# The first microseconds of a transformer kernel: a new order for its first loads

## The reference

```python
for i in range(DEPTH):                      # DEPTH = 4, D_MODEL = 1024, SEQ = 256
    h = rmsnorm(x, norm_mix[i])
    if kind == 0: m = mla_mixer(h, positions, w_in[j], q_norm[j], w_uq[j], kv_norm[j], w_ukv[j], w_o[j])
    ...
    x = x + m
    x = x + sq_relu_mlp(rmsnorm(x, norm_mlp[i]), mlp_w1[i], mlp_w2[i])
return rmsnorm(x, norm_final)

def mla_mixer(h, ...):
    proj = h @ w_in                         # 1024 x (256 + 256 + 64)
    c_q, c_kv, k_pe = jnp.split(proj, [256, 512], axis=-1)
    q = rmsnorm(c_q, q_norm) @ w_uq
    kv = rmsnorm(c_kv, kv_norm) @ w_ukv
    # rotary embedding of q_pe and k_pe, causal softmax attention, then @ w_o
```

## Time and profile before

| | us |
|---|---|
| median of 3 runs | 1314.98 |
| the three runs | 1311.99, 1314.98, 1315.52 |
| span of the profiled execution | 1312.0 |
| TensorE busy | 1286.5 |
| VectorE busy | 891.4 |
| ScalarE busy | 671.6 |
| GpSimd busy | 43.5 |

### The profile page before, as it was taken

How to read it: one execution, slowest core, us unless ns; L and a number is a source line. 1 busy time by engine, 2 the same in 40 slices (tenths; PEclk the granted TensorE clock), 3 DMA queues, 4 the chain that set the end, 5 groups by cost and what they waited for, 6 DMA issues and landing times.

```text
span 1312.0 us, 18369 instructions
## 1 busy us (share of the span) xinstructions
PE 1286.5 (98%) x7578; PEld 1126.3 (86%) x7578; DVE 891.4 (68%) x1180; ACT 671.6 (51%) x861; POOL 43.5 (3%) x58
## 2 busy tenths in 40 slices
PE   6999999999999999999999999999999999999998
PEld 5888888888999888887999888888887888888886
DVE  5877666665666666666899886766667876666664
ACT  5555554444555454444776644544445645454442
POOL 3000000000000000000101110000000000000000
PEclk9999999999999999999999999999999999999999
DMA  9744465555845475545574643755554334565540
GB/s 289 143 168 148 141 232 201 193 192 161 233 149 180 132 254 192 192 165 160 181 222 141 203 149 119 249 191 192 191 180 140 117 130 130 168 231 193 192 161 32
DMA packets 146067, 230.93 MB, mean 176 GB/s; under 512 B 7683, under 2 KB 112429, under 8 KB 145984
## 3 DMA queue, kind: packets, MB, share of 16 engines
q1 hardware_dynamic: 143136, 221.66, 50.8%
q0 software_dynamic: 2848, 8.10, 2.9%
HBM read 227.08 MB, written 2.65 MB: 175 GB/s over the span
## 4 chain that ended last, share of the span: by engine, by line
PE 88%; DVE 7%; DMA 1%; issue 1%; ACT 1%; POOL 1%; SPq 0%; POOLq 0%; DVEq 0%; ACTq 0%
PE bank L982 15%; PE acc L902 12%; PE acc L903 12%; PE acc L906 12%; PE bank L987 8%; PE bank L590 7%; PE bank L591 7%; PE bank L592 7%; DVE wlo L573 2%; PE bank L1402 1%; PE bank L1105 1%; PE bank L795 1%; PE bank L1408 1%; PE bank L1090 1%; DMA raw<-in_mla_w_in 1%
## 5 line engine op out<-in xcount | busy, mean ns | idle before, releaser
L573 DVE TENSOR_TENSOR wlo<-raw,whi 128x2048 fp32r<-128x2048 f32 (+2 forms) x207 | 464.7, 2255 | 139.6 <-ACT whi L557 139.5
L557 ACT ACTIVATE whi<-raw 128x2048 fp32r<-128x2048 f32 (+2 forms) x207 | 386.8, 1879 | 45.8 <-PE acc L906 44.2
L982 PE MATMUL bank<-hsplit,whi 128*128 128x512 f32 x896 | 212.2, 389 | 0.0
L903 PE MATMUL acc<-wlo,uhi 128*128 128x512 f32 x512 | 200.1, 391 | 0.0
L902 PE MATMUL acc<-whi,uhi 128*128 128x512 f32 x512 | 199.6, 390 | 0.0
L982 PEld LDWEIGHTS bank<-hsplit,whi 128*128 128x128 f32 x896 | 168.2, 188 | 34.9
L906 PE MATMUL acc<-whi,ulo 128*128 128x512 f32 x512 | 159.2, 390 | 0.0
L590 PE MATMUL bank<-hsplit,whi 128*128 128x256 f32 (+2 forms) x540 | 154.5, 286 | 0.3 <-DVE xn L1980 0.3
L592 PE MATMUL bank<-hsplit,wlo 128*128 128x256 f32 (+2 forms) x540 | 151.4, 280 | 0.0
L591 PE MATMUL bank<-hsplit,whi 128*128 128x256 f32 (+2 forms) x540 | 151.4, 280 | 0.0
L1027 ACT ACTIVATE relu<-bank 128x512 f32<-128x512 f32 x56 | 33.5, 598 | 188.9 <-PE bank L987 188.9
(11 more groups left out here) (252 smaller groups left out, 1813.4 us busy)
## 6 DMA issues: line engine op xcount, KB each, us to landing
raw<-in_mlp_w SPq DMA_DIRECT2D x128, 1024.0 KB, 5.5
raw<-in_ssd_w_in SPq DMA_DIRECT2D x18, 1024.0 KB, 5.4
raw<-in_mla_w_o SPq DMA_DIRECT2D x16, 1024.0 KB, 4.9
raw<-in_mla_w_ukv SPq DMA_DIRECT2D x8, 1024.0 KB, 5.8
raw<-in_moba_w_qkv SPq DMA_DIRECT2D x16, 512.0 KB, 5.3
raw<-in_ssd_w_out SPq DMA_DIRECT2D x8, 1024.0 KB, 4.9
raw<-in_mla_w_uq SPq DMA_DIRECT2D x8, 768.0 KB, 6.0
raw<-in_mla_w_in SPq DMA_DIRECT2D x4, 1024.0 KB, 7.5
```

The lines of the kernel that those rows point to most:

```text
L557: nc.scalar.activation(whi[:, s, lo:e], raw[:, s, lo:e], ACT.Copy).then_inc(w_hi_done[s], 1)
L573: nc.vector.tensor_tensor(wlo[:, s, lo:e], raw[:, s, lo:e], whi[:, s, lo:e].bitcast(F32), ALU.subtract).then_inc(w_split[s], 1)
L903: nc.tensor.matmul(acc[t][half][:], lh, wl[:, k, n], start=False, stop=False)
L982: nc.tensor.matmul(ps, w[0][:, k, m * P:(m + 1) * P], hflat[:, k].rearrange("p a n -> p (a n)"), start=k == 0, stop=False)
```

## The change

SP sends `ident` ahead of the gain. Unit 0 is loaded by two transfers, rows 0 and 1 of its four row groups with a semaphore of their own (`first_half_loaded`), then rows 2 and 3. Before unit 1 SP waits until the second half of unit 0 has landed, and before unit 2 until unit 1 has landed. ScalarE copies the lower half of unit 0 as soon as that half is there, and this copy stands ahead of the copies of tile 0's transposes. POOL computes the power of tile 1 before it issues `relx`, `onehot` and the first latent gains. TensorE's matmuls of `ident` are five and stand ahead of the first transposes.

```diff
--- before.py
+++ after.py
@@ -145,6 +145,7 @@
         ident_loaded = sem("ident_loaded")
         mask_loaded = sem("mask_loaded")
         x_loaded = [sem(f"x_loaded{t}") for t in range(T)]
+        first_half_loaded = sem("first_half_loaded")
         x_ready = sem("x_ready")
         gain_loaded = sem("gain_loaded")
         ssq_done = sem("ssq_done")
@@ -541,6 +542,12 @@
 
         in_halves = (0, 1) if kinds[0] == "mla" else ()
 
+        def act_first_half(act):
+
+            e = units[0][0] * units[0][1]
+            act.wait_ge(first_half_loaded, 16)
+            nc.scalar.activation(whi[:, 0, :e // 2], raw[:, 0, :e // 2], ACT.Copy).then_inc(half_hi_done, 1)
+
         def act_splits(act, key, ahead=AHEAD):
 
             while split_to["act"] < min(first.get(key, key) + ahead + 1, len(units)):
@@ -553,7 +560,8 @@
                 lo = 0
                 if n in in_halves:
                     lo = e // 2
-                    nc.scalar.activation(whi[:, s, :lo], raw[:, s, :lo], ACT.Copy).then_inc(half_hi_done, 1)
+                    if n:
+                        nc.scalar.activation(whi[:, s, :lo], raw[:, s, :lo], ACT.Copy).then_inc(half_hi_done, 1)
                 nc.scalar.activation(whi[:, s, lo:e], raw[:, s, lo:e], ACT.Copy).then_inc(w_hi_done[s], 1)
                 split_to["act"] += 1
 
@@ -664,6 +672,8 @@
             for t in range(T):
                 if not deferred(j):
                     act_sumsq(act, j, t)
+                if j == t == 0 and in_halves:
+                    act_first_half(act)
                 if j < len(stages):
                     act_tr(act, j, t)
                 if j == 0:
@@ -2181,8 +2191,8 @@
                 sp.dma_start(gbc[:], src.to_broadcast([P, DM])).then_inc(gain_loaded, 16)
 
             sp.dma_start(x[:, 0, :], A["x"][0, tok(0), :]).then_inc(x_loaded[0], 16)
+            sp.dma_start(ident[:], A["c_ident"]).then_inc(ident_loaded, 16)
             gains(0)
-            sp.dma_start(ident[:], A["c_ident"]).then_inc(ident_loaded, 16)
             for n, (a, b, srcs) in enumerate(units):
                 s, k = n % SLOTS, n // SLOTS
                 if n == 1:
@@ -2191,9 +2201,17 @@
                     sp.dma_start(mask[:], A["c_mask"]).then_inc(mask_loaded, 16)
                 if n in stage_unit:
                     gains(stage_unit[n] + 1)
+                if n in (1, 2) and in_halves:
+                    sp.wait_ge(raw_loaded[n - 1], raw_count[n - 1])
                 if k:
                     sp.wait_ge(w_split[s], k)
                 w = b // len(srcs)
+                if n == 0 and in_halves:
+                    for half, landed in enumerate((first_half_loaded, raw_loaded[0])):
+                        rows_of = slice(a // 2 * half, a // 2 * (half + 1))
+                        sp.dma_start(raw[:, 0, :a * b].rearrange("p (a b) -> p a b", a=a)[:, rows_of, :],
+                                     srcs[0][:, rows_of, :]).then_inc(landed, 16)
+                    continue
                 for i, src in enumerate(srcs):
                     if isinstance(src, tuple):
                         off, k_rows, width, src = src
@@ -2230,11 +2248,11 @@
                 pool.dma_start(qkvg[:, i, QR:QR + KVR],
                                A["mla_kv_norm"][i:i + 1, :].to_broadcast([P, KVR])).then_inc(qkvg_loaded[i], 16)
 
+            if 0 in norm_index:
+                pool_norm(pool, 0, [1])
             pool.dma_start(relx[0:BUCKETS, :], A["rel_bias"]).then_inc(rel_loaded, 16)
             pool.dma_start(onehot[:], A["c_onehot"]).then_inc(rel_loaded, 16)
             latent_gains(0)
-            if 0 in norm_index:
-                pool_norm(pool, 0, [1])
             pool.wait_ge(raw_loaded[1], raw_count[1])
             latent_gains(1)
             if "ssd" in kinds:
@@ -2298,9 +2316,9 @@
             te.wait_ge(ident_loaded, 16)
             if "moba" in kinds and not bias_in_mla:
                 pe_bias(te)
+            for _ in range(5):
+                nc.tensor.matmul(acc[0][0][:, 0:P], ident[:], ident[:], start=True, stop=True)
             pe_tr(te, 0, 0)
-            for _ in range(7):
-                nc.tensor.matmul(acc[0][0][:, 0:P], ident[:], ident[:], start=True, stop=True)
             for j, (kind, L, i) in enumerate(stages):
                 if kind == "mlp":
                     pe_mlp(te, j, L)
```

## The result

The changed kernel takes 1317.04 us (median of 11 runs, 1316.05 to 1320.26), the kernel before beside it 1313.65 (median of 11, 1311.74 to 1316.17). The ratio is 1.0025, 95% interval 1.0016 to 1.0035. The change made the kernel slower by about 3.4 us, less than the 0.3% that was taken as the limit of what can be told, but the interval of the ratio lies wholly above 1. The predicted time, 1314.6, was a small gain, and its direction was wrong; the range, 1310.8 to 1318.4, held the measured time.

What follows compares the result with a forecast made beforehand. TensorE was taken as the bound, busy 1286.5 of 1312.0 us, its idle time largely at the start. 1314.98 - 0.35 (scaling earlier) + 0 (unit 2) gave 1314.6 us, range 1310.8 to 1318.4.

Steps and rivals of the forecast that it cites:

- the scaling of tile 1: VectorE's step at the start, at 16.37 us before; a microsecond there was claimed to be a microsecond at the end.
- L, the first half of unit 0: Landing time of the first half of unit 0 at the start: 9.4 us, with ends 8.3 and 10.0.
- L+6.6: Forecast start of the scaling of tile 1, 6.6 us after the first half of unit 0 lands; break-even at 9.8.
- the 0.35 us of gain: The scaling of tile 1 starting at 16.0 instead of 16.37 us; the ends give 14.9 and 16.6.
- The first norm: Gain one place later in SP's queue at the start: 0.2 us of queue, wanted at about 7.2, no cost.
- rival (d): TensorE slow at the start, unit 0's matmuls at 0.43 us: +0.2, or net +2.8 (1317.8) if it lasts; chance 0.08.
- the mild case: Only the first twelve matmuls of unit 0 at 0.43 us, ending at 17.0 against 16.8 for tile 1's transposes: +0.2.
- POOL: Moving tile 1's power ahead gains nothing; `onehot`, issued at about 16.1, lands at 22, wanted at 25.15: no cost.
- The waits, unit 1 and unit 2: SP's waits: unit 1 lands at about 17.0, wanted at about 18.7; unit 2 at 24.0, limit 24.1; cost 0.
- The waits, unit 3: Unit 3 is issued behind SP's second wait; the prediction gave it no landing, no limit and no cost.
- Rival (c): SP's waits idle the DMA engines, unit 2 late: at 26, +1.6 (1316.6); at 29.2, +4.8 (1319.8); chance 0.17.
- The base: Profiled execution of 1312.0 us taken as shortest of three, median 3.0 us above; the sum was carried to 1314.98.

## Why the prediction was wrong, point by point

- **What bounds the kernel, and where a microsecond counts.** Right in part. The idle time does not sit largely at the start: of the 25.5 us, 10.0 lie in the first 30 us (TensorE is busy 20.05 of them). What happens at the start does reach the end, but I took the scaling of tile 1 (16.37) as the one number to watch. That number did not move (16.36), and the kernel became slower all the same: between there and 35 us a second place decides, the turn of the latents.
- **L, the first half of unit 0.** 9.4 forecast, 2.11+8.0 = 10.1 measured, just above the high end of the range (10.0). From it the formula, L+6.6, gives 16.7, and 16.36 was measured: 0.3 us too late, as much as the whole forecast gain, since the `wlo` pair ended at 15.3, L+5.2, where L+5.55 was summed. In the other kernels with halves L was 9.4 to 10.25. Tile 1 of x landed at 12.7, where 12.6 was estimated, so it was no cap. So the 0.35 us of gain did not come. The split of unit 0 was not run by itself; with all of the change but the waits the ratio is 0.9995 (0.9986 to 1.0004), nothing that can be told.
- **The first norm.** I costed the gain's new place at nothing; it landed at 8.84, 1.6 after it was wanted. That it cost nothing is right, and for a reason that the prediction gives for `ident`: ScalarE reads the transposes only after its copy of the half.
- **Matmuls of ident, rival (d).** The twelve matmuls of unit 0 ran at 0.43 throughout, as that rival had it, and unit 0 with tile 1 started 0.75 late (0.2 was forecast for the mild case). But undoing it won nothing as long as unit 3 was late, and without the waits it cost nothing that can be told either. The step was under-sized and not on the path.
- **POOL.** Right: `onehot` was there at 19.7 (issued 16.55, 3.1 to landing), wanted at 25.8.
- **The waits, unit 1 and unit 2.** The forecasts held: unit 1 at 16.4 (17.0 forecast), unit 2 at 22.8 (24.0 forecast, limit 24.1).
- **The waits, unit 3: the step that failed.** The prediction names unit 3 as standing behind the second wait and then gives it neither a landing nor a limit, so the sum holds its lateness at nothing. "All later loads wait for `w_split` and move along" is true from unit 4 on; unit 3 goes into a slot not used before and waits for no split. The runs showed in its place: landing at 29.35 instead of 25.9, and the latents of tile 1 scaled 1.8 us later. Landing and limit could be had from the trace and the code: its landing before (25.9), the squares behind its copy in ScalarE's order, which is in the code, and that before the change the queue had been full until then, so that a microsecond in which the DMA engines idle between waits is a microsecond of later landing. I treated unit 2 as the last one that matters since VectorE took it up at 26.40. Rival (c) had the idle DMA engines right but named the wrong unit for this kernel. Its 1316.6 is close to the measured 1317.04 by luck: it adds 1.9 us for unit 2, which was in time, and leaves out unit 3 and the clock.
- **The clock.** I looked for a slow TensorE only at the start. In the profile the larger part of the loss came at the second idle time, 2.75 us, after which 9.5 us were needed for 7.1 us of work. The fall itself could not have been counted on: it comes in some executions and not in others, in the kernel with unit 3 alone delayed even behind idle times of 0.84 and 1.67 us.
- **The base.** I carried the sum from the span to a median 3.0 us above it. The offset is 1.8 for each run; the rest was the scatter of three runs. It moved the predicted time by about a microsecond, not its sign.
- **The range.** That 1310.8 to 1318.4 held the measured time is luck as far as the mechanism goes. It was made that wide for the scatter of three runs and for rival (d), not for a late unit 3.

What would have shown it: write down for every unit behind an added wait its landing, the engine that waits for it, and the next instruction on that engine. Three units, three lines.

## What to carry to other kernels

Here waits for a landing, put between transfers of a full queue, left the DMA engines partly idle, at 0.65 to 0.70 instead of 1.04 to 1.05 over 10 us, and a later transfer that nothing else held back came 3.4 us later. Before adding such a wait, follow it down to the last transfer that the pause reaches, and at each look at what stands behind its consumer in that engine's order: here one copy without haste held up squares that were urgent. When TensorE's idle time grows, look also at what its granted clock does afterwards.

## What the runs showed of the hardware

- **A transfer that is issued only after a landing starts slowly.** Unit 1, 1 MB issued at 11.46 when of SP's queue only the rest of tile 1 of x was under way (landed at 12.7), took 5.0 us to land, against 9.7 for unit 0 under load. The DMA engines were busy 0.50 of the time from 11.5 to 13.5 us, 0.84 up to 16.4, and 0.03 from there to 17.5, when the next unit began. In six other kernels with halves and the first wait it took 5.0 to 5.2, in the kernel before with the waits 8.0. The Trainium skill, DMA: Bandwidth & Descriptors, section Anatomy of one DMA, fits transfers that GpSimd issues with 2.0 us plus bytes at 436 GB/s, which for 1 MB makes 4.4 us, an estimate. Unit 1 was issued by SP, so this is a comparison and no test; the measured 5.0 decides.
- **The granted clock and the pace of matmuls can disagree.** From 12.5 to 17.5 us the changed kernel's record says 1.00, and the matmuls start 0.43 us apart:

```profile
13.09 0.63 PE L1323 MATMUL bank<-whi,hsplit 128*128 128x512 f32 x1
...
13.52 0.63 PE L1322 MATMUL bank<-whi,hsplit 128*128 128x512 f32 x1
```

  From 36 to 42 us the same pace stands beside 0.50. In the first stretch, too, the products took the time that the pace says. The Trainium skill, TensorE: Matmul & The Clock Gate, Part 1, says that the clock halves after idling; the fall at 35 us, in an idle time of 2.75 us, agrees. The length of the last idle time alone did not decide: the clock held over 2.10 us in three kernels and fell behind the same 2.10 us in a fourth, and it held over 1.67 us in three kernels and fell at 37.1 us, 1.1 us after TensorE was back from 1.67 us of idle time, in the kernel with unit 3 alone delayed.
- **The scatter of this program goes with that clock.** Among the 35 runs of the kernel before beside the last four kernels, those at mean clock 0.999 took 1310.67 to 1311.84 us, those at 0.995 and 0.996 took 1314.43 to 1317.74. Which comes first, a late transfer or a fall of the clock, these numbers do not say. Three runs are too few for a base here.
- **GpSimd's power beside VectorE.** The second power of the latents takes 2.66 us when VectorE's 2.3 us subtraction starts just ahead of it (30.45 and 30.63 in the kernel before), and 0.69 us in the four kernels in which VectorE scales first and is idle meanwhile; the first power takes 0.72 us beside an idle VectorE in every kernel.
